# Residual stream kept in on-chip memory across phases, and MoBA gating issued one step ahead

## The reference

```
for i in range(4):
    hn = rms_norm(x, attn_norm[i])
    x = x + (swa_sink_attention, retention, moba_attention)[i % 3](hn, ...)
    x = x + conv_glu_ffn(rms_norm(x, ffn_norm[i]), ...)
return rms_norm(x, final_norm)
# rms_norm: x * rsqrt(mean(x*x) + eps) * g
# conv_glu_ffn: (silu(causal_conv3(h @ w_a) + conv_b) * (h @ w_b)) @ w_down      D_FF = 2816
# swa: attention over the last 128 tokens, 16 query heads, 4 key heads of 64, a sink per head
# moba: each query attends its own 256-token block (causally) and the 3 earlier blocks
#       whose mean key scores highest against it: gate = q . mean(k of block), top 3
# retention: chunks of 128 tokens, state R carried from chunk to chunk
```

## Time and profile before

| | |
|---|---|
| profiled execution, its own time | 17946.72 us (span of the slowest core 17944.9 us, the other cores from 17809.2 us) |
| TensorE, VectorE, ScalarE busy | 52%, 43%, 20% of the span |
| mean granted TensorE clock of the slowest core | 0.678 |
| device memory read, written | 754 MB, 268 MB |
| MoBA phase (15) | from 7590.7 to 13333.4 us |
| an FFN phase, half 0 (5) | from 1648.3 to 2290.3 us, first matmul of its group 0 at 1733.3 us |
| an FFN phase, half 1 (6) | from 2298.0 to 2952.3 us, first matmul of its group 0 at 2401.1 us |
| a sliding-window attention phase (3) | from 519.5 to 1076.9 us, first score matmul at 575.4 us |

### The profile page before, as it was taken

One profiled execution on the slowest core, in us unless ns is written; L12 is line 12 of the kernel. 1 busy time (PEld: TensorE's weight loads), 2 busy tenths in 40 slices (PEclk: granted clock), 3 DMA queues, 4 the chain that ended last, 5 costly groups with the idle time before them and its releaser, 6 DMA issues. The chain is left out here.

```text
span 17944.9 us, 138797 instructions; the slowest of 8 cores (17809.2 to 17944.9 us)
## 1 busy us (share of the span) xinstructions
PE 9342.9 (52%) x40370; PEld 3826.4 (21%) x41072; DVE 7639.1 (43%) x11586; ACT 3670.8 (20%) x5998; POOL 1522.0 (8%) x1975
## 2 busy tenths in 40 slices
PE   4334966755434867423333344444446694333966
PEld 1111422322222323200111111111112241111422
DVE  5665656243644656532111111010014565666655
ACT  2111111222222111211222222222211112111212
POOL 0222010000000000010000000000000000222000
PEclk7556988877556988855555555555558897655987
DMA  2122132333233222200000000000014213122133
GB/s 79 45 54 56 25 71 69 88 90 91 57 87 75 38 62 63 68 7 5 4 4 3 3 3 3 2 3 2 2 54 98 63 25 93 49 54 56 25 66 105
DMA packets 797103, 827.28 MB, mean 46 GB/s; under 512 B 301968, under 2 KB 542352, under 8 KB 795280
## 3 DMA queue, kind: packets, MB, share of 16 engines
q1 hardware_dynamic: 623136, 613.72, 11.9%
q0 software_dynamic: 173232, 204.65, 7.3%
HBM read 754.23 MB, written 268.44 MB: 57 GB/s over the span
## 5 line engine op out<-in xcount | busy, mean ns | idle before, releaser
L1500 PE MATMUL p15moba_ps<-p15moba_P,p15moba_vg 128*128 128x512 bf16 x2037 | 1195.2, 587 | 2139.9 <-ACT p15moba_P L1491 1612.3
L1510 DVE RECIPROCAL p15moba_rec<-p15moba_ps 64x512 f32<-64x512 f32 x128 | 429.5, 3355 | 4319.8 <-PE p15moba_ps L1500 4006.6
L1491 ACT ACTIVATE p15moba_P<-p15moba_ps 128x512 bf16<-128x512 f32 x2176 | 1299.2, 597 | 4390.1 <-PE p15moba_ps L1486 4390.1
L1486 PE MATMUL p15moba_ps<-p15moba_QA,p15moba_kA 80*128 80x256 bf16 x4352 | 1369.7, 417 | 307.6 <-ACT p15moba_P L1491 159.6
L1500 PEld LDWEIGHTS p15moba_ps<-p15moba_P,p15moba_vg 128*128 128x128 bf16 x2176 | 223.0, 102 | 3266.5 <-issue 3266.5
L1496 POOL TENSOR_TENSOR p15moba_P<-p15moba_P,p15moba_cm_sb 128x512 bf16<-128x512 bf16 x256 | 294.6, 1151 | 5440.2 <-ACT p15moba_P L1491 5440.2
L1486 PEld LDWEIGHTS p15moba_ps<-p15moba_QA,p15moba_kA 80*128 80x128 bf16 x4352 | 536.8, 124 | 721.5 <-issue 721.3
L1448 PE MATMUL p15moba_ps<-p15moba_kmT,p15moba_QA 64*128 64x16 bf16 x512 | 22.9, 171 | 713.3 <-DMA p15moba_QA<-qT 663.2
L311 ACT ACT_TABLE_LOAD x18 | 23.1, 1283 | 1194.4 <-DVE p18ffn_xh_sb L533 245.0
L847 DVE RECIPROCAL p23swa_rec<-p23swa_rec 64x256 f32<-64x256 f32 x128 | 223.6, 1747 | 13.9 <-DVE p23swa_rec L845 0.9
L847 DVE RECIPROCAL p3swa_rec<-p3swa_rec 64x256 f32<-64x256 f32 x128 | 223.6, 1747 | 13.9 <-DVE p3swa_rec L845 0.9
(11 more groups left out here) (645 smaller groups left out, 20001.4 us busy)
## 6 DMA issues: line engine op xcount, KB each, us to landing
p7ret_wblk<-l_w_in POOLq DMA_DIRECT2D x48, 256.0 KB, 10.9
p8ret_wblk<-l_w_in POOLq DMA_DIRECT2D x48, 256.0 KB, 11.4
p1qkv_x_sb<-x SPq DMA_DIRECT2D x32, 256.0 KB, 12.7
p2qkv_x_sb<-x SPq DMA_DIRECT2D x32, 256.0 KB, 11.5
p3swa_x_sb<-x SPq DMA_DIRECT2D x32, 256.0 KB, 11.1
xs_0<-p3swa_x_sb SPq DMA_DIRECT2D x32, 256.0 KB, 4.0
p4swa_x_sb<-x SPq DMA_DIRECT2D x32, 256.0 KB, 10.6
xs_0<-p4swa_x_sb SPq DMA_DIRECT2D x32, 256.0 KB, 4.2
```

The source lines that it names most:

```text
L1486: ins = e.matmul(ps_t[:, hh * 256:(hh + 1) * 256], lhsT=kAs[gl][0:80, j * 128:(j + 1) * 128], rhs=QA[qi][0:80, 2 * hh + par, :], start=Tru ...
L1491: S.op("act", lambda e, Pv=Pv, ps_t=ps_t: e.activation(out=Pv[:, :, :], in_=ps_t[:, :].rearrange("p (h q) -> p h q", h=2), func=AF.Exp, sc ...
L1500: S.op("pe", lambda e, po_t=po_t, Pv=Pv, vsl=vsl, j=j, gl=gl, njt=njt: e.matmul(po_t[:, :], lhsT=vg[gl][:, j, vsl], rhs=Pv[:, :, :].rearra ...
L1510: S.op("dve", lambda e, rc=rc, den=den: e.reciprocal(out=rc, in_=den), reads=[po_b], writes=[recb[par]])
```

## The change

Two things, in one diff.

**Residual stream.** One tensor `x_res` is allocated for the whole program, and every phase uses it as its `x_sb`. The order of the phases is changed so that a half's mixer and its FFN follow one another: sliding-window layers now run qkv, attention and FFN of half 0, and then the same of half 1; retention likewise; in the MoBA layer, after the joint MoBA phase, projection and FFN of half 0 and then of half 1; the final norm of a half follows its last FFN. With that the loads of x in attention (4 phases), retention part 2 (2), FFN (8) and final norm (2) go; those in qkv (6), retention part 1 (2) and output projection (2) stay. The stores of x after the mixers (4 + 2 + 2 phases) and after the two FFNs of the last layer go; the other six FFNs and the final norm still store. Half 0's last two tokens, which half 1 needs for its halo, are written by one DMA to a small tensor `x_tail` at the end of half 0's mixer phase (1024 pieces of 8 bytes), and read back contiguously by half 1's FFN. In the FFN only the norms of the halo and of tile 0 stand ahead of the first group; those of tiles 1 to 3 are issued in group 0, each just before its tile's `AB`.

**MoBA.** The loop body is split into `gate(k)` and `att(k)`; gate(k + 1) is issued before att(k).

```diff
 class Res:
-        self.x_sb = cx.sb("x_sb", [128, NCH, T], F32)
+        self.x_sb = cx.opts.get("x_sb") if cx.opts.get("x_sb") is not None else cx.sb("x_sb", [128, NCH, T], F32)
     def load_x(self, xT_d, queue="sp"):
+        if not self.cx.opts.get("load_x", True):
+            return
     def store_x(self, xT_d, queue="sp"):
+        tail = self.cx.opts.get("tail_out")
+        if tail is not None:
+            S.dma(queue, tail[:, :, :], self.x_sb[:, :, T - 2:T], [self.xb[c][3] for c in range(NCH)], [self.outb], Buf("xtail"))
+        if not self.cx.opts.get("store_x", True):
+            return
...
 def emit_ffn(...):
-    emit_norm(cx, R, Fr.g, Fr.gb, banks["ss"], halo=True)
+    emit_norm(cx, R, Fr.g, Fr.gb, banks["ss"], tiles=(0,), halo=True)
     load_w(0)
     load_w(1)
...
         HALO(gi)
         for tt in range(4):
+            if gi == 0 and tt >= 1:
+                emit_norm(cx, R, Fr.g, Fr.gb, banks["ss"], tiles=(tt,))
             AB(gi, tt)
...
 def build_ffn_launch(...):
-        cx.S.dma("sp", R.xh_sb[:, :, :], xp[:, :, T - 2:T].rearrange("c p t -> p c t"), [], [R.xhb], R.xhb)
+        cx.S.dma("sp", R.xh_sb[:, :, :], cx.io["x_tail"][:, :, :], [], [R.xhb], R.xhb)
...
 def build_moba_launch(...):
-    for qb in range(16):
-        for gl in range(NG):
-            ...   # gate, attention, store
+    gate(0)
+    for k in range(len(iters)):
+        if k + 1 < len(iters):
+            gate(k + 1)
+        att(k)
...
 def build_fused():
+    x_res = es_top.enter_context(nc.sbuf_tensor("x_res", [128, NCH, T], F32))
+    x_tail = scr("x_tail", [128, NCH, 2], F32)
...
+        for h in range(2):
+            mix_opts = {"store_x": False}
+            if h == 0:
+                mix_opts["tail_out"] = x_tail
+            if m == 0:
+                phase("qkv%d" % h, ...)
+                phase("swa%d" % h, build_swa_launch, io, dict(mix_opts, fused=True, half=h, load_x=False))
+            elif m == 1:
+                phase("ret1%d" % h, ...)
+                phase("ret2%d" % h, build_ret2_launch, io, dict(mix_opts, ..., load_x=False))
+            else:
+                phase("oproj%d" % h, build_outproj_launch, ..., dict(mix_opts))
+            phase("ffn%d" % h, build_ffn_launch, io, {"halo": ..., "load_x": False, "store_x": not last})
+            if last:
+                phase("fnorm%d" % h, build_fnorm_launch, ..., {"load_x": False})
```

More of the change, by code:

```diff
@@ L1504, in build_moba_launch, with att @@
+    def att(k):
+        qb, gl = iters[k]
+        qi = k % 2
+        nps = st_["nps"]
+        njt = 2 * (qb + 1)
+        for j in range(njt):
+            own = (j // 2 == qb)
             for par in range(2):
+                ps_t, ps_b = cx.ps[1 + (nps % 4)]
+                pi = nps % 4
+                nps += 1
                 po_t, po_b = cx.ps[5 + par]
-                nlo, dlo = (0, 64) if par == 0 else (64, 0)
-                num = po_t[nlo:nlo + 64, :].rearrange("p (h q) -> p h q", h=2)
@@ new lines, in att @@
+                vsl = slice(64, 192) if par == 0 else slice(0, 128)
+                S.op("pe", lambda e, po_t=po_t, Pv=Pv, vsl=vsl, j=j, gl=gl, njt=njt: e.matmul(
+                    po_t[:, :], lhsT=vg[gl][:, j, vsl], rhs=Pv[:, :, :].rearrange("p h q -> p (h q)"),
+                    start=(j == 0), stop=(j == njt - 1)), reads=[Pb[pi], vgb[gl]], writes=[po_b])
+        oi = k % 2
+        for par in range(2):
+            po_t, po_b = cx.ps[5 + par]
+            nlo, dlo = (0, 64) if par == 0 else (64, 0)
+            num = po_t[nlo:nlo + 64, :].rearrange("p (h q) -> p h q", h=2)
+            den = po_t[dlo:dlo + 64, :].rearrange("p (h q) -> p h q", h=2)
+            rc = rec[par][nlo:nlo + 64, :, :]
+            S.op("dve", lambda e, rc=rc, den=den: e.reciprocal(out=rc, in_=den), reads=[po_b], writes=[recb[par]])
+            S.op("dve", lambda e, num=num, rc=rc, oi=oi, nlo=nlo: e.tensor_tensor(
+                out=oo[oi][nlo:nlo + 64, :, :], in0=num, in1=rc, op=ALU.mult),
+                reads=[po_b, recb[par]], writes=[oob[oi]])
@@ new lines, in att @@
+        if not fused:
+            odst = [oTc[2 * gl + hh, :, qb * 256:(qb + 1) * 256] for hh in range(2)]
+        else:
+            odst = [oH[qb // 8][2 * gl + hh, :, (qb % 8) * 256:(qb % 8 + 1) * 256] for hh in range(2)]
+        S.dma_group("sp", [(odst[hh], oo[oi][:, hh, :]) for hh in range(2)],
+                    [oob[oi]], [outb], oob[oi])
+        st_["nps"] = nps
+    gate(0)
[3 more added lines that the diff above has]
+        att(k)
@@ L1753, in build_fused @@
         w = W[i]
-        if m in (0, 2):
+        last = (i == 3)
+        if m == 2:
             for h in range(2):
@@ L1797, in build_fused @@
             if h == 1:
-                io["x_prev"] = xmid0
-            phase("ffn%d" % h, build_ffn_launch, io, {"halo": "zero" if h == 0 else "prev"})
+                io["x_tail"] = x_tail
+            phase("ffn%d" % h, build_ffn_launch, io, {"halo": "zero" if h == 0 else "prev", "load_x": False, "store_x": not last})
             cur[h] = xo
-    for h in range(2):
-        phase("fnorm%d" % h, build_fnorm_launch, dict(base, xT=cur[h], g=C["gfinal"], xo=OUT[h]))
+            if last:
+                phase("fnorm%d" % h, build_fnorm_launch, dict(base, xT=cur[h], g=C["gfinal"], xo=OUT[h]), {"load_x": False})
+    es_top.close()
     return nc
```

192 lines of the change are left out of this document (79 added, 113 removed).

## The result

The changed kernel takes 17354.43 us (median of ten runs, 17336.32 to 17475.78); the kernel before 17958.47 (twenty runs). The ratio is 0.9667, 95% interval 0.9643 to 0.969: faster, by 604 us. Forecast were 17,335 in a range of 17,150 to 17,520.

| step | forecast | measured | how |
|---|---|---|---|
| MoBA | -128 | -136 | start of phase 15 to start of 16: 5746.2, then 5610.3 |
| FFN, 8 phases | -167 | -187 | start of group 1 after the phase's start, sum: 1603.4, then 1416.3 |
| attention heads, 4 | -138 | -108 | first score after the phase's start, sum: 218.4, then 110.0 |
| retention heads, 2 | -81 | -58 | the same: 140.7, then 83.1 |
| final norm, 2 | -34 | -38 | phase length: 73.5 and 73.1, then 55.3 and 52.9 |

A forecast was written before the change was run, and what follows sets the result against it. No engine bounds the whole kernel; 27 phases between barriers each have their own limit. Gains of 128 + 167 + 138 + 81 + 34 + 65 = 613 us from 17946.7 gave a forecast of 17,335, range 17,150 to 17,520.

The forecast's parts named there:

- MoBA: MoBA phase: the wait for the bias copies goes, plus 10.5 at the start; query and bias waits stay; -128 us.
- FFN: Eight FFN phases: x loads go, but norms of tiles 1 to 3 lie on group 0's path; -167 us.
- attention heads: Start of four sliding-window attention phases: first score earlier by the dropped issue of x, mean 34.4 each; -138 us.
- retention heads: Start of two retention part 2 phases: dropped issue of x, 48.8 each, less about 8.5 for w_out; -81 us.
- final norm: Two final norm phases: without x loads the first store comes at +19.9, 17 earlier each; -34 us.
- The ends: Ends of ten phases: no store of x, or only a small one, before the next phase; -65 us.
- Rival E: Heads bound by small pieces beside the weights: attention and retention give 125 instead of 219, ends 35; 17,460 us; chance 10%.
- B: Norms inside FFN group 0 dearer: every tile period at 48, the FFNs gain nothing; 17,500 us; chance 13%.
- C: Norms inside FFN group 0 cheaper: period 33, FFNs give 335, heads at upper ends; 17,130 us; chance 7%.
- D: TensorE's clock drops at new FFN gaps and stays low: 17,819 us through group 0, 18,235 through group 1; chance 3%.

## Why the prediction was right, and where it was off

MoBA: right, mechanism and size, as the split alone and the two moved parts show (the 8 us above the forecast are in the wait for queries, which fell by 20.5 and not by 10.5); the change's name for it ("issued one step ahead") describes the code and not the time. FFN: right in size, tile by tile within 2 us, but one reason was wrong: I laid the wait of the square to the buffer that norm and conv share. The buffer does hold it, for 0.95 us behind the last Silu (row 2242.47); but with a buffer of its own group 1 still starts at +175 to +178, since ScalarE's order puts the square behind that Silu anyway. The table switch I had put ahead of the square falls ahead of the root: row 2242.47 follows a Silu without one, row 2249.88 shows it, 1.28 us with the root right behind, no drain between; ScalarE had been idle before it. By the Trainium skill ("ScalarE: Activation LUTs", section "What ACT_TABLE_LOAD costs") 1.38 more would follow; this trace does not show it.

Mis-sized were the heads: 108 and 58 where the terms said 138 and 81. The step was right that the weights collide with the small loads, but priced it at nothing for attention's forecast (kept as the lower bound, 80) and at 8.5 a phase for retention; with the weights out of the way the heads came 9 to 15 and 23 to 25 us earlier, more than the missing gain. So the gain without weights, 34.4 and 48.8 a phase, was put too low as well (39.0 and 52.9 with the late weights). The ends gave 82 in place of 65: a phase without stores ends in 1.1 us, where I had taken 2.5, and in half 1's retention the state's store, no longer behind x, is issued 37 us before the phase's end (6235.72) and lands under the last projection:

```profile
6198.83 4.44 SPq L156 DMA_DIRECT2D Rend<-p11ret_Rf  x8
```

The errors cancel, 53 short at the heads against 20 over from the FFN, 17 from the ends, 8 and 4 from MoBA and the final norm, and that is luck. Rival E was this collision at nearly twice its size (94 short at the heads); B and C would have needed tile periods of 48 or 33, and the three of each phase were 39 to 42; in D the clock would have stayed at 0.5 into group 1, and it is 0.96 there (2375 to 2471 in the second FFN phase), after 0.82 in group 0.

## What to carry to other kernels

An operation issued earlier in the code is earlier in time only if it passes the waiting instruction in every queue it uses: here the gate stayed behind a store on one engine, a division on another and a whole attention on the third. It was hidden once its load and its transpose had moved; its operations on VectorE still follow the division, but nothing waits for them there any more. Work put between two blocks of a strict-order engine was added to them here, since its first instruction could not start before the last one of the block; in a row ahead of them, where several engines share it, it was cheaper. When a load goes, ask what other transfer starts in its place.

## What was not expected of the hardware

In some FFN stretches the granted clock of TensorE was neither of its two levels but 0.81, in the profile of the kernel before too and for longer in most of the experiments. A group at 0.81 took 102.7 us in place of 95.9, the time of the same group of the same phase in the changed kernel's profile, where the clock was 0.96. The rows are that group in the kernel with the norms in a row, on core 2 (the slowest) and on core 0; the group in the changed kernel; and a group of the kernel before (windows; columns as above):

```profile
6453.00:6555.00 102.00, 100.70 (x407) 42.08 (x414) 64.98 (x96) 19.77 (x33) 9.90 (x20) 0.81 0.15 21
6453.00:6555.00 102.00, 94.12 (x465) 41.83 (x463) 69.06 (x105) 18.88 (x36) 10.58 (x20) 0.97 0.19 26
```
```profile
6610.00:6700.00 90.00, 81.53 (x363) 35.54 (x362) 61.06 (x92) 17.44 (x31) 8.56 (x16) 0.96 0.13 16
```
```profile
17529.00:17632.00 103.00, 101.69 (x411) 42.47 (x418) 65.23 (x97) 20.34 (x36) 10.59 (x20) 0.81 0.15 21
```

The Trainium skill ("TensorE: Matmul & The Clock Gate", section "Seeing it yourself") tells of a limit that takes a whole die to 13/16 of the clock once three of its cores run dense matmuls. 0.81 is that ratio, but in the window above it did not take a whole die: cores 2 to 5 were at 0.81 and cores 0, 1, 6 and 7 at 0.97, so two of each die (cores 0 to 3, 4 to 7). No run here was made to show the cause.

And the issue of a load by SyncE has no fixed price: one DMA of 256 KB took 21.27 us to issue while 8 MB of float32 weights were under way, and 1.06 in the run where they came later.
